# A hybrid decoder layer on one core: expert weights in six transfers of 2 MB per block instead of twelve of 1 MB

## The reference, cut to what matters

```python
logits = (xf @ w_router + b_router).astype(jnp.float32)
top_v, top_e = lax.top_k(logits, TOP_K)
...
    def expert_block(args):
        xe, e = args
        gu = xe @ w_gu[e] + b_gu[e]
        gate = jnp.minimum(gu[..., 0::2], SWIGLU_LIMIT)
        up = jnp.clip(gu[..., 1::2], -SWIGLU_LIMIT, SWIGLU_LIMIT)
        act = (up + 1.0) * (gate * jax.nn.sigmoid(gate * SWIGLU_ALPHA))
        return act @ w_dn[e] + b_dn[e]
...
out = jnp.zeros((t, d), jnp.float32).at[row_tok].add(
    yb.reshape(n_rows, d).astype(jnp.float32) * row_gate[:, None])
```

## Time and profile before

| | |
|---|---|
| median of three runs | 1655.97 us (1649.51 to 1656.35) |
| the profiled execution | 1653.01 us |
| its span, first to last instruction | 1651.2 us |
| TensorE busy | 1512.3 us (92%) |
| VectorE busy | 1290.6 us (78%) |
| ScalarE busy | 1023.7 us (62%) |
| GpSimd busy | 234.0 us (14%) |
| bytes moved by DMA | 486.13 MB, mean 294 GB/s over the span |
| loads of gate-up halves | 264 of 1 MB, median 8.9 us from issue to landing |
| loads of down halves | 132 of 1 MB, median 10.9 us |

### The profile page before, as it was taken

How to read it: one execution, slowest core, us unless ns; L and a number is a source line. 1 busy time by engine, 2 the same in 40 slices (tenths; PEclk the granted TensorE clock), 3 DMA queues, 4 the chain that set the end, 5 groups by cost and what they waited for, 6 DMA issues and landing times.

```text
span 1651.2 us, 20945 instructions
## 1 busy us (share of the span) xinstructions
PE 1512.3 (92%) x7011; PEld 1246.3 (75%) x7011; DVE 1290.6 (78%) x1237; ACT 1023.7 (62%) x918; POOL 234.0 (14%) x148
## 2 busy tenths in 40 slices
PE   5997779873699999999999999999999999999982
PEld 4876657663578888888888888888888888888872
DVE  6225652347489999999999999999999999999991
ACT  6233432330467777777777777777777777777771
POOL 0000000000102221111221111221111122211120
PEclk9999959965899999999999999999999999999996
DMA  9220030060679999999999999999999999999974
GB/s 341 102 77 26 1 154 0 23 229 8 240 286 380 365 384 388 382 386 379 372 372 386 389 385 379 375 375 379 386 387 387 378 371 373 386 383 390 376 269 127
DMA packets 97611, 486.13 MB, mean 294 GB/s; under 512 B 8153, under 2 KB 8178, under 8 KB 63730
## 3 DMA queue, kind: packets, MB, share of 16 engines
q1 hardware_dynamic: 87186, 448.05, 69.3%
q0 software_dynamic: 10400, 37.75, 8.7%
HBM read 461.65 MB, written 24.12 MB: 294 GB/s over the span
## 4 chain that ended last, share of the span: by engine, by line
PE 87%; issue 5%; DVE 4%; DMA 2%; ACT 1%; SPq 0%; DVEq 0%; POOLq 0%; POOL 0%; ACTq 0%
PE gu_bank L998 16%; PE gu_bank L999 16%; PE gu_bank L1000 16%; PE bank L998 9%; PE bank L999 9%; PE bank L1000 9%; PE gu_bank L1189 2%; PE bank L1196 2%; PE bank L1203 2%; PE gu_bank L1089 1%; PE bank L1113 1%; DVE w_lo L663 1%; PE bank L1211 1%; PE bank L1128 1%; DVE arena L731 1%
## 5 line engine op out<-in xcount | busy, mean ns | idle before, releaser
L663 DVE TENSOR_TENSOR w_lo<-raw,w_hi 128x2048 fp32r<-128x2048 f32 x412 | 935.2, 2291 | 128.5 <-ACT w_hi L460 124.5
L460 ACT ACTIVATE w_hi<-raw 128x2048 fp32r<-128x2048 f32 x412 | 789.4, 1920 | 238.6 <-PE gu_bank L1000 183.6
L998 PE MATMUL gu_bank<-w_hi,turned 128*128 128x512 f32 (+1 forms) x1112 | 435.2, 391 | 7.0 <-DVE turned L917 7.0
L1000 PE MATMUL gu_bank<-w_hi,turned 128*128 128x512 f32 (+1 forms) x1112 | 432.1, 389 | 0.0
L999 PE MATMUL gu_bank<-w_lo,turned 128*128 128x512 f32 (+1 forms) x1112 | 432.0, 389 | 0.0
L998 PE MATMUL bank<-w_hi,turned 128*128 128x512 f32 (+1 forms) x616 | 242.4, 394 | 14.3 <-ACT arena L501 7.3
L998 PEld LDWEIGHTS gu_bank<-w_hi,turned 128*128 128x128 f32 x1112 | 209.6, 189 | 49.5 <-issue 5.8
L1000 PEld LDWEIGHTS gu_bank<-w_hi,turned 128*128 128x128 f32 x1112 | 209.4, 188 | 43.0
L999 PEld LDWEIGHTS gu_bank<-w_lo,turned 128*128 128x128 f32 x1112 | 209.7, 189 | 41.8
L999 PE MATMUL bank<-w_lo,turned 128*128 128x512 f32 (+1 forms) x616 | 240.4, 390 | 0.0
L1000 PE MATMUL bank<-w_hi,turned 128*128 128x512 f32 (+1 forms) x616 | 239.8, 389 | 0.0
(11 more groups left out here) (188 smaller groups left out, 1278.0 us busy)
## 6 DMA issues: line engine op xcount, KB each, us to landing
raw<-in_w_gate_up_dram SPq DMA_DIRECT2D x264, 1024.0 KB, 8.9
raw<-in_w_down_dram SPq DMA_DIRECT2D x132, 1024.0 KB, 10.9
raw<-in_w_in_dram SPq DMA_DIRECT2D x10, 1024.0 KB, 7.7
arena<-in_x_dram SPq DMA_DIRECT2D x2, 2048.0 KB, 11.2
raw<-in_w_out_dram SPq DMA_DIRECT2D x4, 1024.0 KB, 5.1
raw<-in_w_mem_kv_dram SPq DMA_DIRECT2D x2, 1024.0 KB, 9.0
arena<-in_position_tables_dram SPq DMA_DIRECT2D x1, 2048.0 KB, 19.6
sum_rows<-arena SPq DMA_DIRECT2D x1, 2048.0 KB, 6.6
```

Source lines behind the costliest of these rows:

```text
L460: a.activation(w_hi[:, slot, :], raw_ap, ACT.Copy).then_inc(hi_ready, 1)
L663: v.tensor_tensor(w_lo[:, slot, :], raw_ap, w_hi[:, slot, :].bitcast(F32), ALU.subtract).then_inc(lo_ready, 1)
L998: pe.matmul(bank, a[0], b[0], start=first, stop=False)
L1000: return pe.matmul(bank, a[1], b[0], start=False, stop=last)
```

## The change

Each pair of neighbouring halves (k0 and k1, k2 and k3, and so on) is fetched by one DMA of 2 MB into two neighbouring slots of `raw`. The DMA increments the semaphore of the even slot alone. SyncE issues it once both slots are free, so it waits for the low part of the half that sat in the odd slot (`8 + k` where it was `7 + k`). ScalarE waits for the even half and the odd half alike on the semaphore of the even slot, at the same value. What ScalarE, VectorE and TensorE do with a half, and in what order, is as it was. The first halves of the first block, before the loop, are paired as well.

```diff
         def raw_value(i):
 
-            return 16 * ((4 if i % 6 < 4 else 0) + i // 6 + 1)
+            even = i - i % 2
+            return 16 * ((4 if even % 6 < 4 else 0) + even // 6 + 1)
...
-                sp.dma_start(raw[:, i % 6, :].rearrange("p (e n) -> p e n", e=1),
-                             gu_dram[bass.ds(e, 1), :, k, :]
-                             .rearrange("e p n -> p e n")).then_inc(raw_in[i % 6], 16)
+                sp.dma_start(raw[:, i % 6:i % 6 + 2, :],
+                             gu_dram[bass.ds(e, 1), :, k:k + 2, :]
+                             .rearrange("e p k n -> p (e k) n")).then_inc(raw_in[i % 6], 16)
...
-                sp.dma_start(raw[:, i % 6, :].rearrange("p (k n) -> p k n", k=2),
-                             dn_dram[bass.ds(e, 1), :, 2 * j:2 * j + 2, :]
+                sp.dma_start(raw[:, i % 6:i % 6 + 2, :].rearrange("p i (k n) -> p (i k) n", k=2),
+                             dn_dram[bass.ds(e, 1), :, 2 * j:2 * j + 4, :]
                              .rearrange("e p k n -> p (e k) n")).then_inc(raw_in[i % 6], 16)
 
 
-            for k in range(4):
-                gate_up(0, k, k, 13 + k)
+            for k in (0, 2):
+                gate_up(0, k, k, 14 + k)
             sp.wait_ge(mix_lo, 2 * NT)
             sp.wait_ge(pv_done, NR)
             gate_up(0, 4, 4)
-            gate_up(0, 5, 5)
...
-            gate_up(0, 6, 6, 17)
-            gate_up(0, 7, 7, 18)
+            gate_up(0, 6, 6, 18)
...
-                for k in range(GU):
-                    gate_up(e, k, GU + k, b * 12 + (7 + k))
-                for j in range(DN):
-                    down(before, j, 2 * GU + j, b * 12 + (7 + GU + j))
+                for k in range(0, GU, 2):
+                    gate_up(e, k, GU + k, b * 12 + (8 + k))
+                for j in range(0, DN, 2):
+                    down(before, j, 2 * GU + j, b * 12 + (8 + GU + j))
             e = sp.value_load(exp_i[0:1, bass.ds(loops, 1)], min_val=0, max_val=E - 1)
-            for j in range(DN):
-                down(e, j, GU + j, loops * 12 + (19 + j))
+            for j in range(0, DN, 2):
+                down(e, j, GU + j, loops * 12 + (20 + j))
...
-                   raw_in[i % 6], value if b is None else (b - 1) * 32 + value)
+                   raw_in[i % 6 // 2 * 2], value if b is None else (b - 1) * 32 + value)
```

## The result

The change makes the kernel slower: 1759.59 us in the median of four runs (1758.30 to 1773.62), against 1652.81 us for the kernel before in its four runs (1649.51 to 1656.35). The ratio is 1.066, with a 95% interval of 1.061 to 1.070. The profiled execution took 1758.3 us, with a span of 1756.5 us, so it is 105.3 us above the profiled 1653.0 us of before. The forecast was 1740 us, within 1680 to 1775.

A forecast was written before the change was run, and what follows sets the result against it. TensorE was taken as the bound at 35.8 us a block; a closed chain of waits through the loads would take 38.8, so 30 blocks x 3.0 less 2.3 gives +88 us: 1740 us, range 1680 to 1775.

The forecast's parts named there:

- Step 1: From k1's split to the first half of k6/k7 being through: about 785.0 instead of 782.8, 2.2 us late.
- Step 2: From k6's landing to k11's, the five halves still take 18.0 us; the last pair is there at 803.0.
- the correction of -0.6 us: After GpSimd's scatter, with both halves of each pair queued, some idle DMA time is used: 0.6 us less a block.
- Steps 3 and 4: ScalarE takes k10 3.2 us late; 4.24 us to its split's end, then VectorE runs 11.7 us without pause.
- The bound of 39.4: High bound in us for a block, if none of the DMA's idle time is used: 1759 us in all.
- Where TensorE stalls: Mostly ahead of k0: a margin of 2.3 us is used once, then 3.0 us are lost a block.
- The other pairs: k0/k1 (808.0, needed by 812.6) and k4/k5 (819.9, needed by 821.4) land in time, so add nothing.
- The clock: If each stall halves TensorE's clock, its own work is 37.5 us a block, under 38.8: no further cost.
- The cover holds: Rival: indirect traffic yields when the weight queue is full; chain 36.0 us, time within 0.5% of 1655; chance 0.08.
- partly: Rival: the slow DMA stretch comes from thin queues; chain of 36.3 to 37.4 us, 1668 to 1700 us; chance 0.12.
- Larger transfers are cheaper: Rival: each load carries a gap on the DMA engines and six go; 1645 to 1653 us; chance 0.05.
- Worse than forecast: Rival: k4/k5 late too, or stall and slow clock delay copies; 40 us or more a block, 1765 to 1800; chance 0.07.

The follow-up runs named there:

- gate-up kernel: Against the kernel before, only the gate-up halves (k0/k1 to k6/k7) are loaded as pairs, the down halves singly: 1652.0 us, ratio 0.998 to 1.003.
- down pairs: Against the kernel before, only the down halves (k8/k9, k10/k11) are loaded as pairs, the gate-up halves singly: 1756.2 us, ratio 1.061 to 1.066.
- late issue: Against the kernel before, still 1 MB loads, but the even half is issued only once the odd slot is free too: 1682.1 us, ratio 1.011 to 1.025.
- shared landing: Against the kernel before, 1 MB loads issued as before, but ScalarE takes an even half only when the odd one has landed: 1700.9 us.
- pairs k0/k1 to k4/k5 with k8/k9: Against the kernel before, these four pairs go as 2 MB loads, k6, k7, k10 and k11 singly: 1730.4 us, ratio 1.044 to 1.056.
- the gather ahead: Against the whole change, the gather for the block after next goes ahead of the scatter on GpSimd's queue: 1731.8 us, 38.3 us a block.

## Why the prediction was right

- **What bounds the kernel.** Right. TensorE had no slack, and nothing on the side of the loads could gain: in no kernel is a block of the steady loop shorter than 35.8 us.
- **Step 1, k6/k7 issued late.** Right: 7.5 us from issue to landing, against 4.9 + 2.5 + 0.4 = 7.8, so 0.3 us too much.
- **Step 2, the five halves behind.** From the issue of k6/k7 to the landing of k10/k11 the forecast had 4.9 + 18.0 + 0.4 - 0.6 = 22.7 us. The block shown has 22.5, but over all blocks the way from the end of k1's split to k10's copy is 23.4 us in the mean, where the forecast has 0.2 + 22.7 = 22.9. This is the term that was too small, and by more than 0.5 us, since step 1 hides 0.3 of it. The part that fits is the correction of -0.6 us: the lull was not filled, as k8/k9 were asked for later too. It is filled when down halves go singly.
- **Steps 3 and 4, ScalarE and VectorE.** Right to 0.02 us: from k10's copy to the end of the next k1's split the change has 15.96 us in the mean, and so have the kernels with its waits on k6 and k10, against 4.24 + 11.7 = 15.94.
- **The sum.** 39.3 us a block against 38.8. With 0.5 us more in each of 30 blocks the forecast of +88 becomes +103; +105 was measured. The bound of 39.4 held for the mean, though single blocks reach 39.9. The forecast did not know the late gather, whose move ahead gives 1.0 us a block back; the block came out near because the 18.0 us of step 2 were measured with the gather's bytes in them.
- **Where TensorE stalls.** Right in place and near in size: once a block ahead of k0, 2.1 us of 2 to 3. A stall for gathered rows of 1.1 us a block, and one of 0.7 us for a down half, were not foreseen.
- **The other pairs.** That k0/k1 and k4/k5 have cover is right: they cost nothing in the gate-up kernel. k8/k9, for which no cover was worked out, do cost: they hold ScalarE, they leave the DMA short, and they bunch VectorE.
- **The clock.** The forecast allowed for a stall that brings the clock down, as in the earlier trace rows, and said that it would cost nothing more while the chain leads. It did not come down: 1.00 from the second block on in the change, with matmuls idle for 1.7 us ahead of k0. It did fall with stalls of 4 us (down pairs). It had no part in the result of the change.
- **The rivals.** "The cover holds" and "partly" are out by 39.3 us. "Larger transfers are cheaper" is out by the kernel with 1 MB loads and the same waits, which was not slower than the change. "Worse than forecast" named the pair k4/k5, which had nothing to do with it.
- **A reading.** "From the twelfth slice on" is too wide for the DMA, whose twelfth slice is a 7, and the last slices of both are below 9. The windows by block, on which the forecast rests, are not touched.

What is not shown: which part of the 1.0 us that the gather ahead gives back is the wait for rows and which is its traffic; and why k8/k9 run at 367 GB/s between k6/k7 and the scatter. GpSimd's issue is under way in that stretch, but no run separates it.

## What to carry to other kernels

Merging two loads delays the first and hides it until the second has landed; before doing so, follow one closed chain from slot freed to slot freed, through every in-order engine, and compare its length with the period of the engine that leads. In the kernel before the chain was 39.0 - 2.2 - 2.5 = 34.3 us, by the forecast's terms, and so 1.5 us shorter than the period of 35.8. Such a margin can be lost, and more, to a change that leaves bytes and slots alone. When an experiment hits the predicted time, look at its blocks too: a mean of 36.8 us can be a row of 35.8 with a few of 42.

## What the runs showed of the hardware

- GpSimd's issue of an indirect DMA took from 1.8 to 10.6 us for the same 128 rows (2.1 in the kernel before, 8.4 in the change), and ended 1.47 to 1.51 us after the end of VectorE's run of subtractions with both inputs in SBUF.
- In four kernels (late issue, shared landing, down pairs, pairs k0/k1 to k4/k5 with k8/k9) TensorE's matmuls stood for 3.1 to 4.7 us in 36 blocks of the loop. Each of these 36 blocks has a stretch at a granted clock of 0.50, and no other block from the third on has one in any of the kernels, though others stood for up to 1.7 us. Ahead of the loop, a stall of 0.99 us was followed by such a stretch.
- A load of 2 MB with no other under way (k6/k7 of the change; the DMA's share is 0.00 in the microsecond after its issue) landed after 7.5 us. Loads of 1 MB just ahead of the full loop took 4.7 to 5.3 us.
